# Last expert's results added by products with a 0/1 matrix, with its weight units in another order

## The reference

```python
idx, w_sel = top-2 experts of the token and their weights, normalised to sum 1
combine = (one_hot(idx, 16) * w_sel[..., None]).sum(1)
for e in range(16):
    he = silu(hf @ w_gate[e]) * (hf @ w_up[e])
    y = y + combine[:, e:e + 1] * (he @ w_down[e])
h = layer_norm(2 ** 0.25 * h1 + y, ln2_g, ln2_b)
```

## Time and profile before

| | us |
|---|---|
| three runs | 867.91, 867.13, 863.42 (median 867.13) |
| the profiled execution, its own time | 863.86 |
| its span | 861.9 |
| TensorE busy | 751.6 (87%) |
| VectorE busy | 588.9 (68%) |
| ScalarE busy | 424.6 (49%) |

### The profile page before, as it was taken

The page is one execution under the profiler, slowest core; times in us unless marked ns, Lnnn a source line. Parts: engine busy times, 40 slices in busy tenths (PEclk is TensorE's granted clock), DMA queues, the critical chain, the costliest instruction groups (busy, mean ns, idle before and its releaser), DMA issues.

```text
span 861.9 us, 10746 instructions
## 1 busy us (share of the span) xinstructions
PE 751.6 (87%) x3961; PEld 605.7 (70%) x3963; DVE 588.9 (68%) x794; ACT 424.6 (49%) x490; POOL 103.5 (12%) x118
## 2 busy tenths in 40 slices
PE   3399999998998777999999875899999999999920
PEld 1396899985576446887888764688888888888720
DVE  5806999795255744211464868888898988988838
ACT  5343244245433646222122131678878778777712
POOL 4640000000000000000000111211111112112012
PEclk9999999999998989999999975999999999999965
DMA  8636222300070300135226973699999999996143
GB/s 194 198 122 220 67 85 87 111 1 1 1 247 1 98 1 1 49 98 195 69 80 241 410 260 121 236 379 398 399 387 402 396 398 396 389 405 236 62 183 130
DMA packets 102540, 167.09 MB, mean 194 GB/s; under 512 B 18848, under 2 KB 39584, under 8 KB 102504
## 3 DMA queue, kind: packets, MB, share of 16 engines
q1 hardware_dynamic: 95024, 145.53, 47.6%
q0 software_dynamic: 4752, 13.11, 3.9%
q10 hardware_dynamic: 2728, 7.95, 2.4%
HBM read 156.07 MB, written 17.42 MB: 201 GB/s over the span
## 4 chain that ended last, share of the span: by engine, by line
PE 78%; DVE 8%; ACT 6%; issue 4%; DMA 2%; SPq 1%; POOL 1%; POOLq 0%; DVEq 0%; ACTq 0%
PE low L1007 15%; PE low L1009 15%; PE low L1008 15%; PE wide L1007 7%; PE wide L1009 7%; PE wide L1008 7%; PE wide L1356 2%; ACT prob L840 2%; PE low L1177 1%; ACT w_hi L650 1%; PE wide L1162 1%; PE low L1308 1%; PE low L1240 1%; SPq L393 1%; PE low L1174 1%
## 5 line engine op out<-in xcount | busy, mean ns | idle before, releaser
L1726 DVE TENSOR_TENSOR m_lo<-m_raw,m_hi 128x2048 fp32r<-128x2048 f32 x95 | 214.9, 2290 | 28.8 <-ACT m_hi L886 28.1
L886 ACT ACTIVATE m_hi<-m_raw 128x2048 fp32r<-128x2048 f32 x95 | 179.7, 1917 | 26.0 <-PE low L1009 26.0
L1447 DVE TENSOR_TENSOR w_lo<-raw,w_hi 128x2048 fp32r<-128x2048 f32 x28 | 64.1, 2291 | 80.9 <-ACT w_hi L650 80.6
L1007 PE MATMUL low<-m_hi,xe_hi 128*128 128x512 f32 x256 | 103.9, 406 | 3.6 <-DVE xe_lo L1791 3.2
L1007 PE MATMUL low<-hT_hi,w_hi 128*128 128x512 f32 (+1 forms) x240 | 93.6, 390 | 10.6 <-issue 10.6
L1009 PE MATMUL low<-m_hi,xe_lo 128*128 128x512 f32 x256 | 100.8, 394 | 0.0
L1008 PE MATMUL low<-m_lo,xe_hi 128*128 128x512 f32 x256 | 100.4, 392 | 0.0
L1008 PE MATMUL low<-hT_lo,w_hi 128*128 128x512 f32 (+1 forms) x240 | 93.2, 388 | 0.0
L1009 PE MATMUL low<-hT_hi,w_lo 128*128 128x512 f32 (+1 forms) x240 | 92.7, 386 | 0.0
L650 ACT ACTIVATE w_hi<-raw 128x2048 fp32r<-128x2048 f32 x28 | 53.4, 1908 | 17.8 <-PE wide L1009 8.3
L1007 PEld LDWEIGHTS low<-hT_hi,w_hi 128*128 128x128 f32 x240 | 46.8, 195 | 20.6 <-issue 11.0
(11 more groups left out here) (341 smaller groups left out, 1458.9 us busy)
## 6 DMA issues: line engine op xcount, KB each, us to landing
m_raw<-in_w_gate SPq DMA_DIRECT2D x32, 1024.0 KB, 7.5
m_raw<-in_w_up SPq DMA_DIRECT2D x32, 1024.0 KB, 7.6
m_raw<-in_w_down SPq DMA_DIRECT2D x31, 1024.0 KB, 8.6
raw<-in_w_in SPq DMA_DIRECT2D x19, 1024.0 KB, 5.2
raw<-in_w_out SPq DMA_DIRECT2D x4, 1024.0 KB, 4.9
table_dram<-table_row ACTq DMA_DIRECT2D x1, 2624.0 KB
strips<-table_dram SPq DMA_DIRECT2D x8, 264.0 KB, 4.0
xn<-in_x SPq DMA_DIRECT2D x4, 512.0 KB, 5.0
```

The costliest lines, as they stand in the source:

```text
L886: nc.scalar.activation(m_hi[n % MS][:, :], (m_spare if is_last(n, j) else m_raw[slot])[:, :], ACT.Copy).then_inc(q["m_hi_ready"], 1)
L1007: nc.tensor.matmul(outp, lh, rh, start=first, stop=False)
L1447: v.tensor_tensor(w_lo[:, u % SPL, :], raw[:, u % RAW, :], w_hi[:, u % SPL, :].bitcast(F32), ALU.subtract).then_inc(q["lo_ready"], 1)
L1726: v.tensor_tensor(m_lo[n % MS][:, :], (m_spare if is_last(n, j) else m_raw[n % MR])[:, :], m_hi[n % MS][:, :].bitcast(F32), ALU.subtract). ...
```

## The change

Expert 15's result is no longer scattered. It stays on the chip, scaled by each token's weight (`e_scale`) and split into `yl_hi` and `yl_lo`; a 0/1 matrix (`last_selT`, slots by tokens, made by comparing each token's rank in expert 15's list with the slot numbers and transposed on TensorE) brings its rows to the tokens in a product. The second expert's results (y2) are added in the same accumulation, by a product with a diagonal matrix of their weights (`second_w`). y1 times its weight plus h1 is made ahead on VectorE (`part`). `combine` is then one addition. Rows of `y_dram` that nobody writes must be zero, so zeros are written to it early. The loads of y1 and y2 begin when expert 14's scatter has landed, all on SP's queue. In the order of units, down 14 comes before up 15. Some semaphores of the power -1/2 steps are merged into `var_ready` and `rstd_ready`, each wait with the same producer. The y1 and y2 tiles lie in slots 0 to 3 of the weight ring instead of at its foot.

```diff
@@ SP
+            sp.dma_start(y_dram.rearrange("(a p) d -> a p d", p=P),
+                         zero_rows.rearrange("(o p) d -> o p d", o=1).to_broadcast([2 * TT, P, D])).then_inc(q["load_late"], 16)
             for u in range(U_GATE + 2, NU):
                 load(u)
...
-            for e in range(1, NE):
+            for e in range(1, NE - 1):
                 order += [(e, 0), (e, 1), (e, 2), (e, 3), (e - 1, 4), (e - 1, 5)]
-            order += [(NE - 1, 4), (NE - 1, 5)]
+            e = NE - 1
+            order += [(e, 0), (e, 1), (e - 1, 4), (e - 1, 5), (e, 2), (e, 3), (e, 4), (e, 5)]
...
+            sp.wait_ge(q["all_scattered"], 1)
+            sp.wait_ge(q["m_lo_ready"], MU * NE - MR + 4)
+            for i in range(TT):
+                    sp.dma_start(y2[:, i, :], y_dram[S + i * P:S + (i + 1) * P, :]).then_inc(x_loaded[i], 16)
+                    sp.dma_start(y1[:, i, :], y_dram[i * P:(i + 1) * P, :]).then_inc(x_loaded[i], 16)
@@ GpSimd
             pool.wait_ge(q["y_out"], 2)
+            pool.wait_ge(q["load_late"], 16 * 11)
             scatter(0, 5, 0)
...
-            for e in range(NE - 3, NE):
+            for e in range(NE - 3, NE - 1):
...
-            pool.wait_ge(scattered[(NE - 1) % 2], 16 * NE // 2)
+            pool.wait_ge(scattered[(NE - 2) % 2], 16 * NE // 2)
+            pool.sem_inc(q["ye_free"], 1)
+            pool.sem_inc(q["all_scattered"], 1)
             over = pool.value_load(most[0:1, 0:1], min_val=0, max_val=S)
@@ ScalarE
+            hd_hi_out(NE - 2)
+            for i in range(3):
+                m_split_hi(MU + i, NE // 2 - 1)
+            silu_gate(NE - 1, MU * NE - 6)
+            m_split_hi(MU + 3, NE // 2 - 1)
+            result_out(0, MU * NE - 4, NE - 1)
+            m_split_hi(MU + 4, NE // 2 - 1)
+            m_split_hi(MU + 5, NE // 2 - 1)
+            hd_hi_out(NE - 1)
+            act.wait_ge(q["sel_done"], 1)
+            nc.scalar.activation(e_scale[:, :], bank[7][:, 0:1], ACT.Copy)
+            nc.scalar.activation(last_selT[:, :, :], bank[6][:, :].rearrange("p (i x) -> p i x", i=TT), ACT.Copy).then_inc(q["sel_out"], 1)
...
             for half in range(2):
                 act.wait_ge(q["m_used"], MU * NE - 1 + half)
-                nc.scalar.activation(ye[1][:, half * 512:half * 512 + 512], bank[4 + half][:, :], ACT.Copy).then_inc(q["y_out"], 1)
+                nc.scalar.activation(yl_hi[:, half * 512:half * 512 + 512], bank[4 + half][:, :], ACT.Copy, scale=e_scale[:, 0:1]).then_inc(q["yl_hi_ready"], 1)
...
-            for i in range(TT):
-                act.dma_start(y2[:, i, :], y_dram[S + i * P:S + (i + 1) * P, :]).then_inc(x_loaded[i], 16)
@@ TensorE
+            u = MU * NE - 7
+            pe.wait_ge(q["xe_lo_ready"], NE)
+            m_unit(u, 1, bank[0][:, :], 0, xe_hi, xe_lo)
+            m_unit(u + 1, 2, bank[0][:, :], 1, xe_hi, xe_lo)
+            pe.wait_ge(q["hd_lo_ready"], NE - 1)
+            pe.wait_ge(q["y_out"], NE - 1)
+            m_unit(u + 2, 0, bank[4][:, :], None, hd_hi, hd_lo)
+            m_unit(u + 3, 1, bank[5][:, :], None, hd_hi, hd_lo)
+            m_unit(u + 4, 2, bank[1][:, :], 0, xe_hi, xe_lo)
+            m_unit(u + 5, 0, bank[1][:, :], 1, xe_hi, xe_lo)
+            pe.wait_ge(q["sel_ready"], 1)
+            for i in range(TT):
+                nc.tensor.transpose(bank[6][:, i * P:(i + 1) * P], last_sel[:, i, :], ident[:, :])
+            for i in range(TT):
+                mm = nc.tensor.matmul(bank[7][:, 0:1], last_sel[:, i, :], e_weight[:, i:i + 1], start=(i == 0), stop=(i == TT - 1))
+            mm.then_inc(q["sel_done"], 1)
+            hidden(NE - 1)
             pe.wait_ge(q["hd_lo_ready"], NE)
             pe.wait_ge(q["y_out"], NE)
...
+            def closing_sum(i):
+                pair = (wide[1], low[0], low[1], wide[0])[i]
+                pe.wait_ge(x_loaded[i], 48)
+                for half in range(2):
+                    nc.tensor.matmul(pair[:, half * 512:half * 512 + 512], second_w[:, i, :], y2[:, i, half * 512:half * 512 + 512], start=True, stop=False)
+                for half in range(2):
+                    pe.wait_ge(q["yl_lo_ready"], half + 1)
+                    o = pair[:, half * 512:half * 512 + 512]
+                    nc.tensor.matmul(o, last_selT[:, i, :], yl_hi[:, half * 512:half * 512 + 512], start=False, stop=False)
+                    mm = nc.tensor.matmul(o, last_selT[:, i, :], yl_lo[:, half * 512:half * 512 + 512], start=False, stop=True)
+                mm.then_inc(q["sum_done"], 1)
@@ VectorE, after the router
+            step(v.tensor_copy(e_rank[:, :].rearrange("p (i o) -> p i o", o=1), t3[:, :, NE - 1:NE]))
...
+            step(v.tensor_tensor(as3(e_weight[:, :]), as3(weight[:, 0, :]), one1[:, :, NE - 1:NE], ALU.mult))
+            step(v.tensor_tensor(gm, as3(weight[:, 1, :]), one2[:, :, NE - 1:NE], ALU.mult))
+            step(v.tensor_tensor(as3(e_weight[:, :]), as3(e_weight[:, :]), gm, ALU.add))
             hidden_out(0, 4)
@@ VectorE, at the end
+            hd_lo_out(NE - 2)
+            for i in range(3):
+                m_split_lo(MU + i, j)
+            dve.wait_ge(q["m_lo_ready"], MU * NE - 4)
+            v.tensor_tensor(last_sel[:, :, :], ... slot numbers == e_rank ...).then_inc(q["sel_ready"], 1)
+            for i in range(3, 5):
+                m_split_lo(MU + i, j)
+            hidden_out(NE - 1, MU * NE - 2)
+            v.tensor_tensor(second_w[:, :, :], ... ident * weight[:, 1, :] ...).then_inc(q["sel_ready"], 2)
+            hd_lo_out(NE - 1)
+            m_split_lo(MU + 5, j)
+            def part(i, count):
+                dve.wait_ge(x_loaded[i], count)
+                v.scalar_tensor_tensor(out=y1[:, i, :], in0=y1[:, i, :], scalar=weight[:, 0, i:i + 1], in1=h1[:, i, :], op0=ALU.mult, op1=ALU.add).then_inc(q["part_ready"], 1)
+            def last_lo(half):
+                at_half = slice(half * 512, half * 512 + 512)
+                dve.wait_ge(q["yl_hi_ready"], half + 1)
+                v.scalar_tensor_tensor(out=yl_lo[:, at_half], in0=bank[4 + half][:, :], scalar=e_scale[:, 0:1], in1=yl_hi[:, at_half].bitcast(F32),
+                                       op0=ALU.mult, op1=ALU.subtract).then_inc(q["yl_lo_ready"], 1)
+            part(0, 48)
+            part(1, 48)
+            last_lo(0)
+            part(2, 48)
+            last_lo(1)
+            part(3, 48)
             over = dve.value_load(most[0:1, 0:1], min_val=0, max_val=S)
...
             def combine(i):
-                dve.wait_ge(x_loaded[i], 48)
-                step(v.scalar_tensor_tensor(out=h1[:, i, :], in0=y1[:, i, :], scalar=weight[:, 0, i:i + 1], in1=h1[:, i, :], op0=ALU.mult, op1=ALU.add))
-                v.scalar_tensor_tensor(out=h1[:, i, :], in0=y2[:, i, :], scalar=weight[:, 1, i:i + 1], in1=h1[:, i, :], op0=ALU.mult, op1=ALU.add).then_inc(q["combined"], 1)
+                dve.wait_ge(q["sum_done"], i + 1)
+                dve.wait_ge(q["part_ready"], i + 1)
+                v.tensor_tensor(h1[:, i, :], (wide[1], low[0], low[1], wide[0])[i][:, :], y1[:, i, :], ALU.add).then_inc(q["combined"], 1)
```

More of the change, by code:

```diff
@@ L245, in build @@
         o_hd = at("o_hd", [P, F // P, P], F32, 40)
-        y1 = at("y1", [P, TT, D], F32, A0)
-        y2 = at("y2", [P, TT, D], F32, A0 + 16)
+        y1 = at("y1", [P, TT, D], F32, A0 + 32)
+        y2 = at("y2", [P, TT, D], F32, A0 + 48)
+        last_sel = at("last_sel", [P, TT, P], F32, A0 + 88)
+        last_selT = at("last_selT", [P, TT, P], F32R, A0 + 90)
+        second_w = at("second_w", [P, TT, P], F32, A0 + 92)
+        e_rank = at("e_rank", [P, TT], F32, A0 + 144.5)
+        e_weight = at("e_weight", [P, TT], F32, A0 + 144.5 + 1 / 32)
+        e_scale = at("e_scale", [P, 1], F32, A0 + 144.5 + 1 / 16)
+        yl_hi = at("yl_hi", [P, D], F32R, 52)
+        yl_lo = at("yl_lo", [P, D], F32R, 32)
         g2 = at("g2", [P, D], F32, A0 + 80)
@@ L942, in _, with expert_act @@
             m_split_hi(5)
-            def expert_act(j, s, last=False):
+            def expert_act(j, s):
                 e, n = j * 2 + (1 + s), MU * (1 + s)
@@ L951, in expert_act @@
                 m_split_hi(n + 3, j)
-                if not last:
-                    xe_hi_out(e + 1)
+                xe_hi_out(e + 1)
                 m_split_hi(n + 4, j)
                 m_split_hi(n + 5, j)
-                if last:
-                    hd_hi_out(e)
                 result_out(s, j * MR + (n + 4), j * 2 + (1 + s))
@@ L980, in _ @@
                     nc.scalar.activation(ye[0][:, :], wide[0][:, :], ACT.Copy).then_inc(q["o_act"], 1)
-            act.wait_ge(q["all_scattered"], 1)
-            for i in range(TT):
-                act.dma_start(y2[:, i, :], y_dram[S + i * P:S + (i + 1) * P, :]).then_inc(x_loaded[i], 16)
             for i in range(TT - 1):
@@ L1384, in _, with expert_pe @@
             hidden(0)
-            def expert_pe(j, s, last=False):
+            def expert_pe(j, s):
                 e, n = j * 2 + (1 + s), MU * (1 + s)
```

(35 more changed lines are left out.)

79 lines of the change are left out of this document (42 added, 37 removed).

## The result

| | before | changed kernel |
|---|---|---|
| executions, us | 867.91, 867.13, 863.42, 863.1 | 859.12, 856.25, 855.54, 853.51 |
| median | 865.27 | 855.89 |
| profiled execution, its span | 863.86, 861.9 | 859.12, 857.3 |
| TensorE, VectorE, ScalarE busy, us | 751.6, 588.9, 424.6 | 766.2, 592.0, 425.1 |

The ratio is 0.9893, with an interval of 0.9845 to 0.9941: 9.4 us less by the medians, where the prediction had 7.5 less and 858.0. The sign was right, and 855.89 lies inside the range. One of the 22 executions of the kernel before on that chip took 4154.85 us, and the ratio leaves it out.

A forecast was written before the change was run, and what follows sets the result against it. The prediction took the chain of waits in the last 37 us, with TensorE idle, as the place to gain: 3.95 + 1.33 + 2.64 - 0.4 = 7.5 us less than the mean 865.6, predicted 858.0, range 852.5 to 863.5.

The forecast's parts named there:

- down 15 starts: TensorE's last down product, expert 15: starts at 819.95 on the old axis, 1.1 us later, with `hid` uncovered.
- loads of y start: Eight loads of y1 and y2 on SP's queue: issued at 817.4 on the old axis, 13 us earlier.
- last pair there: Last pair of y1 and y2 loads: lands 12.4 us after the loads' start, at 829.8 on the old axis.
- branch on VectorE: Branch on `most` ahead of VectorE's first combine: costs between 0 and 1.1 us, taken as 0.49.
- first combine: VectorE's combine 0: starts at 831.6 against 835.55 on the old axis, 3.95 us won.
- first combine to VectorE's end: VectorE's closing stretch: 19.4 us where it was 23.3, shorter combines saving 1.33 and 2.64 us.
- a closing sum: TensorE's closing products for one tile: 2.65 us, hidden, with little to spare at first.
- lost ahead of T by small products: Three four-column products on VectorE after the weights, ahead of expert 0's `hid`: 0.4 us lost.
- zeros on the queue: Writing 4.19 MB of zeros on SP's queue at 241.7: 10.9 us, hidden under 25 us of cover.
- A: Rival at the first combine: TensorE, not the loads, sets its start; 2.9 us more gained, 855; chance 0.12.
- B: Rival at TensorE's closing sums: half clock, 5.3 us a tile, up to 4 us lost, 862; chance 0.10.
- C: Rival at the y loads: scatter of 14 or its signal late, only 3.6 us won, 862; chance 0.08.

The follow-up runs named there:

- e1: The changed kernel with the eight loads of y1 and y2 waiting for the very last low half; 859.96 us, ratio 0.9945 to the kernel before.
- e3: The changed kernel with both low halves right behind parts 0 and 1, parts 2 and 3 behind combines 0 and 1; 852.92 us, ratio 0.9866.
- e4: The changed kernel with the units in the old order, down 14 behind up 15; 862.21 us, ratio 0.9974 to the kernel before.
- g3: The kernel e3 measured again, unchanged, on another chip; 852.41 us, ratio 0.9891 to the kernel before.
- e2: The changed kernel with the zeros written a second time, to another tensor in HBM, on the same queue; 865.82 us, ratio 1.0022.

## Why the prediction was right, point by point

All times from T (816.62 on the axis that the prediction used).

| step | predicted | measured |
|---|---|---|
| down 15 starts | +3.3 | +3.30 |
| scatter of expert 14 issued | -3.3 | -3.37 |
| loads of y start | +0.8 | -0.04 |
| last pair there | +13.2 | +13.3 |
| branch on VectorE | 0.49 | 0 |
| first combine | +15.0 | +14.6 |
| first combine to VectorE's end | 19.4 | 19.2 |
| a closing sum | 2.65 | 2.65 |
| lost ahead of T by small products | 0.4 | 0.3 |
| zeros on the queue | 10.9 | 18.2 |

**What held.** The claim that carried the number: VectorE waits for the last pair ahead of the first combine, so that 13 us of earlier loads bring only 4. The chain, e1 and e3 agree on it. The shorter combines brought 4.1 us from the first combine to VectorE's end (23.3 to 19.2), 3.97 foreseen. `hid` is exposed to the tenth foreseen. The sum behind T was 7.9 and measured 8.4, and 0.3 were lost just ahead of T: 8.1 in all, inside the bounds of 5.3 to 8.3 that the prediction gave the forecast. Ahead of T TensorE waited 1.52 us for expert 0's `hid` instead of 0.96 and 0.56 for `xe_lo` instead of 0.84.

**Three errors that nearly cancelled.** The loads began 0.8 us sooner. From the issue of a scatter to its signal on GpSimd is 3.29 us in both kernels, but behind that came 1.00 us before and 0.04 now: the whole 1.00 hung on the branch, not only the 0.49 that the row of the sequencer shows and of which I took half. The branch on VectorE, priced at 0.49, cost nothing, as it was read beneath the running `part` 3. The last pair landed 13.4 us after the start of the loads, not 12.4. The bulk of the traffic ended 11.8 us after it as before (see the windows below), and the landing came later, with the packet of code among the loads (see e1), which the prediction didn't have. Together the three make 0.4 us. That the last pair's time fits to a tenth is luck: its two terms were off by 0.8 and 1.0 in opposite directions.

**The size of the zeros** was the worst term. I priced 4.19 MB at 384 GB/s, the rate of the table's copy. That rate was bytes by the queue's share of 16 engines' time, so by busy time, and busy time isn't elapsed time. A window of the changed kernel with the zeros under way (clock, DMA share and GB/s come last):

```profile
258.00:266.00 8.00, 8.00 (x37) 6.46 (x36) 4.38 (x17) 0.60 (x1) 2.69 (x1) 1.00 0.51 207
```

The DMA engines are busy for 0.51 of the time and move 207 GB/s: per busy time that is 406, near the 384, and by elapsed time it is half of that. The 18.2 and 19.6 us of the two writes come to 230 and 214 GB/s. The Trainium skill (DMA: Bandwidth & Descriptors, Latency and other measured facts) gives 207 to 214 GB/s for copies between tensors in HBM at a friendly row pitch; by that figure 4.19 MB are an estimated 20 us, and the trace agrees. The cover was mis-sized too, the other way: unit 14 had landed by 250.35 and not only by 254, so it was 29 us and not 25. The margin was 11 us where the prediction had 14, and the outcome is the same.

**The rivals.** *A*: TensorE would have been next by 2.8 us (e3's combine 0 at T + 11.8), the 2.9 that the prediction gave. It isn't the bound, as the windows over the loads' end show:

```profile
830.00:831.00 1.00, 1.00 (x4) 0.38 (x2) 0.00 (x0) 0.18 (x1) 0.00 (x0) 1.00 1.01 414
...
832.00:833.00 1.00, 0.00 (x0) 0.00 (x0) 1.00 (x2) 0.00 (x0) 0.00 (x0) 1.00 0.12 49
```

The loads run at 414 GB/s almost to the end. The Trainium skill (DMA: Bandwidth & Descriptors, Where 436 GB/s comes from) would have them bound at 358; the trace disagrees here as it did before. *B*, closing sums at half clock: not in the changed kernel (1.00 in both rows above), but in e1, where combine 1 waited 1.91 us for TensorE. There TensorE had stood idle for 2.48 and for 1.80 us inside tile 0's sum, in the changed kernel for 1.67 once. In e4 it was so too: the clock was 0.50 up to 839, where tile 1's sum ends, and combine 1 waited 2.53. Even so it cost next to nothing: from the first combine to the end 22.0 us in e1 and 22.6 in e4, 22.3 in the changed kernel, as the clock was back for the later tiles. The loss of up to 4 us that the rival named was not there, the 0.3 that the prediction held against it fits. *C*: the loads got ahead. e4 is what C would have been, and it won 2.1 us by the medians and 1.6 by T to end, not the 3.6 foreseen: I had not counted that VectorE then still asks for the last pair ahead of the first combine.

## What to carry to other kernels

Moving a transfer ahead is worth only what its last consumer in the queue lets through: look for the instruction that needs the last landing and stands in front of the path, and move it behind. Here that order was worth 2.2 us more in one profile and 1.0 in another, and the work moved (2.6 us) cost 0.45 in its new place.

An edit that pays nothing alone may be what the rest lives on: the swap of units by itself gave 1.0008, the rest without the swap 0.9974, both 0.99.

Read a gain from the stage that it lies in, measured from a fixed event. The two profiled executions differed by 4.7 us, with 8.4 won behind T and 3.5 lost where the change has nothing.

## What the runs showed of the hardware that was not expected

- **Writes from HBM to HBM left the DMA engines idle about half of the time (share 0.51 at 207 GB/s), and the loads behind them on the same queue waited.** 4.19 MB of zeros held the next load back by 18.2 us, a second such write by 19.6 more: 230 and 214 GB/s.
- **A 16 KB packet of the program's code among the loads went with a last landing about 1 us later**, 13.3 to 13.8 us after their start in nine profiles against 12.2 to 12.6 in four without it.
- **The granted clock falls in a hole of TensorE's work, in some executions of one kernel and not in others.** TensorE is idle for 1.41 us ahead of down 15 each time, and four of eight profiles went to 0.50 (1.2 GHz) as down 15 began, and were back at 1.00 about 3 us later, at a price of 1.4 to 1.6 us. Neither profile with the old order fell there (before and e4, idle for 1.65 and 0.42 us), where down 14 fills the wait ahead of the transposes of `hid`. No profile of the changed kernel has the fall; by an estimate from TensorE's 2.8 us to spare it would cost nothing there, and in e3's order it costs all of it (first combine at T + 13.3 in g3, + 11.8 in e3). The Trainium skill (TensorE: Matmul & The Clock Gate, What's actually happening) has the throttled state as the default, released by activity; the traces agree in that each fall here follows a hole, and show besides that the same hole doesn't always do it.
- **The same stage runs at another mean clock from run to run**: 0.83 to 0.95 between 280 and 350 us over all profiles of this study, and with it 10 us from the earliest to the latest time (349.0 to 359.5) of one conversion behind it. The latest of these is e2's, where the zeros add to it.
- **A branch on a value read from memory cost VectorE nothing while its last instruction ran.** It lay beneath 1.28 us of `part` 3; on GpSimd, which had nothing else to do, it had delayed the next signal by 1.0 us.
